# Group sums and S5 products reordered at the start, the fourth modulation group read behind the recurrence, and both layers' memory keys and values computed before the first FFN

## The chip, the cores and the metric

The kernel runs on one core of a Trainium2 chip. The metric is the device time of one execution in microseconds. A profiled execution gives a span and a record of every instruction and transfer; the times of this text come from there unless they are called medians.

## The reference

Two transformer blocks work on 512 tokens of 1024 channels. The first is modulated by a vector c, and mixes with four branches (RWKV-7, spatial gating, short convolution, S5). The second has two layers of attention with 12 heads, and 4 heads more that attend to 256 memory tokens. Cut to what matters:

```python
mod = silu(c) @ ada_w + ada_b                     # 1024 x 6144
sh1, sc1, gt1, sh2, sc2, gt2 = split(mod, 6)
h = rms_norm(x, g1) * (1 + sc1) + sh1
p = h @ w_in
merged = sum(sigmoid(gate_i) * branch_i(p))       # four branches
x = x + gt1 * (merged @ w_o)
h = rms_norm(x, g2) * (1 + sc2) + sh2
x = x + gt2 * (relu(h @ ffn_w1) ** 2 @ ffn_w2)
x = rms_norm(x, final_g)
for layer in (0, 1):                              # fox attention, dilated attention
    xn = rmsnorm(x, norm_mix[layer])
    mn = rmsnorm(mem, norm_mem[layer])            # 256 memory tokens
    q, k, v, qm = split(xn @ w_in_2[layer])       # layer 0: and the forget logits
    km, vm = split(mn @ w_mem_kv[layer])
    heads = concat(attention(q, k, v), softmax(qm @ km.T / 8) @ vm)
    x = x + heads @ w_out[layer]
    x = x + conv_ffn(rmsnorm(x, norm_ffn[layer]))
out = rmsnorm(x, norm_final)
```

## The kernel before

**Products.** Activations lie channels by tokens, in eight k-blocks of 128 channels. A product is split: each weight and each activation is a high and a low part, and three matmuls (w_hi h_hi, w_hi h_lo, w_lo h_hi) stand for one. A weight piece has 1024 columns of 128 rows; for a tile of 128 channels by 512 tokens it gives 24 matmuls (L1617). POOL loads pieces in a fixed order into four slots: w_hi by one transfer two pieces ahead (L442), a negated copy (L448), then a second transfer that adds the weight to it (L451), which makes w_lo. The first load waits until DVE has used two modulation blocks (L453). PE's tiles go through four banks of PSUM in turn; each is freed by the engine that reads it.

**Modulation.** The 1024 x 6144 matrix comes as 48 blocks of 512 KB, eight for each of the six groups. SP issues them in program order among its other transfers (L352, L357). Blocks 0 to 3 go to PE directly (L1690). For all others DVE multiplies a block by a column of silu(c) and adds it to a running sum (L576, L578 in `modulate(group, a, b)`); a MEMSET (L580) marks the end of a group; PE adds the sum over the partitions (L1682, `modulation`); DVE adds the bias (L587). Eight slots hold the first 16 blocks. Blocks 8 to 11 wait until PE has taken a slot, 12 to 15 until DVE has.

**Opening.** ACT squares x, PE adds the squares (L1841), DVE takes the reciprocal (L527). DVE then makes the S5 tables by complex products (L1009 to L1014), the last with 1024 columns, which is the S5 filter f; PE transposes it (L1850) and multiplies it (L1855). After the first two groups the norm gives h_hi (ACT) and h_lo (DVE, L534), and PE makes ten tiles of the projection: bg, cg, z of the convolution, gating and S5. DVE reads group 2 between those tiles, makes the convolution's y (L1062 to L1065), then the S5 tables (L1076 to L1092), then the spatial gating: means (L1098), squares (L1101), which PE adds (L1873), the root, and normed values (L1106) that PE multiplies (L1879). Then the S5 inputs (L1899), the RWKV recurrence, and the gates.

**Behind the recurrence.** SP issues blocks 24 to 27 when the recurrence is over, then x anew as each pair of merged tiles is ready (L412), then blocks 28 to 47. Each gated tile is a PE product, then L1127 and L1136 on DVE; the merged tiles go through w_o, eight tiles. `mixer_update(k)` (L1188) adds tile k to x and reads two blocks, of groups 3 and 4. The sums of group 3 stand on PE before w_o's last tile, those of group 4 after it, then the squares of x (L1698), and the FFN with four groups of 16 tiles.

**Heads of the two attention layers.** PE makes memq0, memq1, q0, k0, v0, then memk0, memk1, memv0, memv1: 256 columns wide, from `memory_norm` on DVE (L836, L483, L484, eight times), which norms the memory for that layer; memT is loaded for each layer. memv tiles are copied by ACT and turned by PE (L1711), and copied by DVE (L822). In the first layer DVE also makes the forget parts (L858 to L867) there. In the second q0 and k0 are rotated (L805 to L807, PE turns them by L1708). Attention starts with the memory heads: scores (L1782), maxima (L890), exponentials, turns (L1797), outputs (L1811); the other projections run beside it. The squares of the memory are made beside the last FFN groups before each layer.

The order of the work is written out by hand: each engine runs its own program, and semaphores hold it.

Of the kernel before, what the change touches and what calls it, by code (L numbers as in the profile page):

```python
# [43 lines left out]
ADA_PE, ADA_FIRST = 4, 8  # L44


def ada_landed(q):

    if q < 16:
        return f"ada_in{q % ADA_FIRST}", 16 * (q // ADA_FIRST + 1)  # L50
    return f"ada_in{q % ADA}", 32 + 16 * ((q - 16) // ADA + 1)
# [3 lines left out]
N_KV = 4  # L55


def down_pieces(first):

    pairs, cols, at = set(), {}, first  # L60
    for n_in in (N_FOX, N_DIL):
        at += n_in + N_KV
# [66 lines left out]
HEAD_PIECES = ["memq0", "memq1", "q0", "k0", "v0", "memk0", "memk1", "memv0", "memv1"]  # L129
# [22 lines left out]
def turned_pieces(layer):  # L152

    return [name for name in HEAD_PIECES + BESIDE_PIECES if name[0] == "v" or name[:4] == "memv" or (layer and name[0] in "qk")]
# [18 lines left out]
def build(nc, A, out):  # L173
    n_mixer = sum(n for _, n in mixer_pieces())
    n_block1 = n_mixer + 8 + 2 * 8 * FF_GROUPS
    small_extra = 3 * sum(n for what, n in mixer_pieces() if what.endswith("_out"))
    pair_first, piece_cols = down_pieces(n_block1)
    first_beside = n_block1 + small_extra + 1 + len(HEAD_PIECES)
# [9 lines left out]
    pieces = n_block1 + sum(n + N_KV + 8 + 2 * FF2 + 8 * len(FF2_GROUPS) for n in (N_FOX, N_DIL))  # L188
    with ExitStack() as ctx:
# [80 lines left out]
        first_slots = [arena[:, at:at + D] for at in [base_at + D * i for i in range(ADA_FIRST - 2)] + [4096, 4096 + D]]  # L270
# [40 lines left out]
        mem_in = at_m["p"].rearrange("p a b c -> p (a b c)")[:, 0:KT * MT].rearrange("p (k t) -> p k t", k=KT)  # L311
# [5 lines left out]
        room = at_m["pt"].rearrange("p a b c -> p (a b c)")  # L317
        mem_sq = lambda k: room[:, MT * (k % 2):MT * (k % 2) + MT]
        mem_t = lambda k: room[:, MT * (2 + k % 2):MT * (2 + k % 2) + MT]
        mem_total, mem_rstd = room[:, 4 * MT:5 * MT], room[:, 5 * MT:6 * MT]  # L320
# [11 lines left out]
        def mn(pair, k):  # L332

            return pair[:, k // 2, MT * (k % 2):MT * (k % 2) + MT]
# [4 lines left out]
        def _(sp):  # L339
# [22 lines left out]

# [7 lines left out]
            for q in range(16, 24):  # L370
                ada_piece(q, ada_second["ada"])
# [1864 lines left out]
```

## Time and profile before

| | us |
|---|---|
| median of the runs (lowest to highest, 3 runs) | 2261.84 (2259.82 to 2265.03) |
| the profiled execution | 2262.56 |
| its span | 2260.7 |
| PE busy | 2124.0 (94%) |
| DVE busy | 1296.8 (57%) |
| POOL busy | 841.6 (37%) |
| ACT busy | 455.7 (20%) |

The mean granted clock of PE was 0.968 of full speed. A profile lists busy time and, before a group of instructions, the idle time of its engine with what ended it. An engine that is not the bound may be idle without a price; what counts is which wait ends last in a stretch. A busy PE is not always a fast one, since its clock has two levels, 1.2 and 2.4 GHz.

### The profile page before, as it was taken

To read this page: it belongs to the slowest core of one execution; us is meant where nothing else is said; L and a number is where in the kernel's file an instruction comes from. 1 tells how busy PE (TensorE), PEld (TensorE's weight loads), DVE (VectorE), ACT (ScalarE), POOL (GpSimd) and SP (SyncE) were. 2 spreads that over 40 slices of the span, in tenths; PEclk is the share of its full clock that TensorE was granted. 3 is DMA by queue.
4 is the path that set the end of the run, shared out by engine and by line. 5 is a ranking of instruction groups with operands and counts; after the bars stand their busy time and mean duration, and the time that the engine had idled before them with its cause. 6 is when DMAs were issued, how large, how long until landed. Compare 5 with 4: busy or idle time off the path is not lost.

```text
span 2260.7 us, 27381 instructions
## 1 busy us (share of the span) xinstructions
PE 2124.0 (94%) x10790; PEld 1684.3 (75%) x10790; DVE 1296.8 (57%) x1827; ACT 455.7 (20%) x839; POOL 841.6 (37%) x1009
## 2 busy tenths in 40 slices
PE   6989799998799999998999999999989989999996
PEld 5768587776588888876777888888766768888885
DVE  6775646437653243684444754727746657727374
ACT  2112301220100000313333211202224342202021
POOL 1323233233244444442223444444432224444442
PEclk7999899999799999999999999999999999999998
DMA  8867567579799888875556888988964549889885
GB/s 289 229 139 170 112 142 165 114 168 234 210 241 198 190 193 195 190 170 119 110 103 162 186 192 198 186 197 171 200 135 99 112 90 195 189 196 197 190 187 127
DMA packets 121783, 389.34 MB, mean 172 GB/s; under 512 B 25220, under 2 KB 27396, under 8 KB 121272
## 3 DMA queue, kind: packets, MB, share of 16 engines
q0 software_dynamic: 96624, 346.27, 70.6%
q1 hardware_dynamic: 25032, 41.32, 5.5%
q8 instruction: 86, 1.41, 0.3%
q14 instruction: 41, 0.34, 0.0%
HBM read 383.67 MB, written 3.92 MB: 171 GB/s over the span
## 4 chain that ended last, share of the span: by engine, by line
PE 77%; DVE 14%; DMA 6%; issue 1%; ACT 1%; POOL 0%; SPq 0%; DVEq 0%; ACTq 0%
PE ps L1617 64%; DMA w_lo<-in_w 2%; DMA arena<-in_ada 2%; PE ps L1646 2%; PE ps L1782 2%; PE ps L1811 2%; PE ps L1797 1%; DVE work L690 1%; PE ps L1969 1%; DVE g_lo L484 1%; PE ps L1733 1%; DVE arena L691 1%; DVE arena L578 1%; DMA w_hi<-in_w 1%; DVE small L890 0%
## 5 line engine op out<-in xcount | busy, mean ns | idle before, releaser
L1617 PE MATMUL ps<-h_hi,w_hi 128*128 128x512 f32 x1760 | 711.8, 404 | 27.3 <-DVE h_lo L534 13.1
L1617 PE MATMUL ps<-h_hi,w_lo 128*128 128x512 f32 x1760 | 690.3, 392 | 0.0
L1617 PE MATMUL ps<-h_lo,w_hi 128*128 128x512 f32 x1760 | 690.2, 392 | 0.0
L442 POOL DMA_DIRECT2D w_hi<-in_w x334 | 186.3, 558 | 1218.1 <-PE ps L1617 1082.9
L1617 PEld LDWEIGHTS ps<-h_hi,w_hi 128*128 128x128 f32 x1760 | 333.0, 189 | 125.5 <-issue 29.9
L1617 PEld LDWEIGHTS ps<-h_hi,w_lo 128*128 128x128 f32 x1760 | 332.8, 189 | 71.5
L1617 PEld LDWEIGHTS ps<-h_lo,w_hi 128*128 128x128 f32 x1760 | 333.8, 190 | 65.0 <-issue 2.2
L448 POOL TENSOR_SCALAR w_lo<-w_hi 128x1024 fp32r<-128x1024 f32 (+1 forms) x334 | 355.6, 1065 | 67.1 <-DMA w_hi<-in_w 61.8
L451 POOL DMA_DIRECT2D w_lo<-in_w x334 | 300.9, 901 | 106.0 <-POOL w_lo L448 106.0
L1617 PE MATMUL ps<-g_hi,w_hi 128*128 128x512 f32 (+1 forms) x760 | 297.1, 391 | 10.3 <-DMA w_lo<-in_w 6.3
L1617 PE MATMUL ps<-g_lo,w_hi 128*128 128x512 f32 (+1 forms) x760 | 291.1, 383 | 0.0
L1617 PE MATMUL ps<-g_hi,w_lo 128*128 128x512 f32 (+1 forms) x760 | 291.0, 383 | 0.0
L1617 PEld LDWEIGHTS ps<-g_hi,w_hi 128*128 128x128 f32 x760 | 144.8, 191 | 43.9 <-DMA w_lo<-in_w 9.2
L1617 PEld LDWEIGHTS ps<-g_hi,w_lo 128*128 128x128 f32 x760 | 144.7, 190 | 27.8
L1617 PEld LDWEIGHTS ps<-g_lo,w_hi 128*128 128x128 f32 x760 | 144.9, 191 | 26.6 <-issue 0.5
L1575 ACT ACTIVATE arena<-arena,vec 128x512 f32<-128x512 f32 x88 | 71.8, 816 | 392.1 <-DVE arena L936 388.8
L950 DVE TENSOR_TENSOR x<-ps,x 128x512 f32<-128x512 f32 x48 | 33.2, 692 | 146.0 <-PE ps L1617 135.8
L941 DVE SCALAR_TENSOR_TENSOR arena<-arena,vec 128x511 f32<-128x511 f32 x88 | 114.9, 1305 | 3.3 <-ACT arena L1575 0.3
L936 DVE TENSOR_TENSOR arena<-ps,work 128x512 f32<-128x512 f32 x88 | 60.8, 691 | 90.3 <-PE ps L1617 88.9
L1205 DVE TENSOR_TENSOR arena<-arena 128x512 f32<-128x512 f32 x32 | 54.3, 1696 | 70.6 <-ACT arena L1496 70.6
L1213 DVE SCALAR_TENSOR_TENSOR x<-ps,mod,x 128x512 f32<-128x512 f32 x32 | 24.0, 751 | 101.9 <-PE ps L1617 101.7
L483 DVE CAST g_hi<-arena 128x512 fp32r<-128x512 f32 (+1 forms) x100 | 75.5, 755 | 3.4
(376 smaller groups left out, 2109.3 us busy)
## 6 DMA issues: line engine op xcount, KB each, us to landing
w_hi<-in_w POOLq DMA_DIRECT2D x318, 512.0 KB, 3.9
w_lo<-in_w POOLq DMA_DIRECT2D x318, 512.0 KB, 5.6
arena<-in_ada SPq DMA_DIRECT2D x40, 512.0 KB, 9.4
w_hi<-in_w POOLq DMA_DIRECT2D x16, 384.0 KB, 3.4
w_lo<-in_w POOLq DMA_DIRECT2D x16, 384.0 KB, 5.1
x<-in_ada SPq DMA_DIRECT2D x8, 512.0 KB, 7.9
x<-in_xT SPq DMA_DIRECT2D x1, 2048.0 KB, 9.5
x<-in_xT SPq DMA_DIRECT2D x4, 512.0 KB, 5.3
```

Source lines behind the costliest of these rows:

```text
L442: pool.dma_start(w_hi[:, q % SLOTS, 0:n], A["w"][q][:, 0:n]).then_inc(S(f"high_in{q % SLOTS}"), 16)
L448: pool.tensor_scalar(w_lo[:, q % SLOTS, 0:n], w_hi[:, q % SLOTS, 0:n].bitcast(F32), -1.0, 0.0, ALU.mult, ALU.add).then_inc(S("negated"), 1)
L451: pool.dma_start(w_lo[:, q % SLOTS, 0:n], A["w"][q][:, 0:n], accum_op=ALU.add).then_inc(S(f"low_in{q % SLOTS}"), 16)
L483: do(dve.tensor_copy(hi, src))
L936: do(dve.tensor_tensor(cv_m["z"][:, side, :], tile()[:], rstd, ALU.mult), "conv_scaled")
L941: do(dve.scalar_tensor_tensor(dst[:, 1:], z[:, :T - 1], w(1), dst[:, 1:], ALU.mult, ALU.add))
L1205: do(dve.tensor_tensor(s, r, r, ALU.mult), "relu_used")
L1575: do(act.activation(c[:, j % 2, :], cv_m["z"][:, side, :], ACT.Identity, scale=V("cw2", at), bias=V("cb2", 44 * layer + 22 * side + j0 + j ...
L1617: mm = pe.matmul(bank, w[:, slot, cols], a(k), start=(k == 0 and i == 0), stop=(k == blocks - 1 and i == 2))
L1646: mm = pe.matmul(banks[i], w[:, slots[i], cols], a(k), start=(k == 0 and j == 0), stop=(k == blocks - 1 and j == 2))
L1782: mm = pe.matmul(ps[2 + g][:, 0:width], at_m["q"][half(g), pair, P * qb:P * qb + P], keys, start=True, stop=not fox)
L1811: mm = pe.matmul(ps[6][64 * g:64 * g + 64, P * qb:P * qb + P], values, at_m["pt"][:, u % 2, g, P * b:P * b + P], start=(b == 0), stop=(b = ...
```

## The change

1. **Opening.** Eleven blocks have their own slots and are issued at once; the other five wait for DVE's reads alone. DVE's filter product stands behind the norm, `modulate(1)` ahead of the reciprocal. PE makes three tiles of the projection before the S5 transposes (other banks) and one between those and the S5 products.
2. **Group 2.** Blocks 16 to 19 are issued at h_ready, 20 to 23 behind the S5 transfers. DVE reads them beside the S5 and RWKV steps; the convolution's y moves into the gating's waits; PE's sums of the group, in a bank of the tiles, stand ahead of the gate projections.
3. **Group 3.** Blocks 24 to 27, memT and 28 to 31 are issued behind the recurrence; DVE reads the group after o_normed and after rw_out. x is loaded behind them. `mixer_update(k)` reads one block, of group 4.
4. **Memory.** Both layers' memory keys and values are made between w_o and the first FFN, from one load of memT. The factor 1/rms of a memory token is applied afterwards: to keys on DVE, in the first FFN group; to values by ACT as it copies them. Values are made tokens by channels, so nothing is turned. The heads lose memory_norm, four pieces, their copies and turns; v0's turn moves into attention.

The core of the diff:

```diff
-ADA_PE, ADA_FIRST = 4, 8
+ADA_PE, ADA_FIRST = 4, 11
...
             for q in range(16):
-                if ADA_FIRST <= q < ADA_FIRST + ADA_PE:
-                    sp.wait_ge(S("ada_taken"), q - ADA_FIRST + 1)
-                elif q >= ADA_FIRST + ADA_PE:
-                    sp.wait_ge(S("ada_used"), q - ADA_FIRST - ADA_PE + 1)
-                sp.dma_start(first_slots[q % ADA_FIRST], A["ada"][q]).then_inc(S(ada_landed(q)[0]), 16)
+                if q >= ADA_FIRST:
+                    sp.wait_ge(S("ada_used"), q - ADA_FIRST + (3 if q == 15 else 1))
+                sp.dma_start(first_slots[first_room(q)], A["ada"][q]).then_inc(S(ada_landed(q)[0]), 16)
...
             def memory_root():
                 need("rms_ready")
                 do(dve.reciprocal(mem_rstd, mem_rstd))
+                for i in range(2):
+                    do(dve.tensor_tensor(mem_m["diag"], mem_rstd[:, P * i:P * i + P], K("ident"), ALU.mult))
+                    do(dve.tensor_reduce(mem_row[:, i:i + 1], mem_m["diag"], AX.X, ALU.add), "mem_row")
+            def memory_low(i):
+                layer, k = i // KT, i % KT
+                need("mem_high")
+                do(dve.scalar_tensor_tensor(mn(g_lo, layer, k), mem_in[:, k, :], V("g_mem2", 8 * layer + k), mn(g_hi, layer, k).bitcast(F32),
+                                            ALU.mult, ALU.subtract), "mem_ready")
...
-            complex_product(f, (by_step(0, 0), by_step(1, 0)), (by_channel(bb[:, 0]), by_channel(bb[:, 1])), blocks4(tmp))
...
             modulate(0, ADA_PE, 8)
+            modulate(1, 0, 8)
             norm_start()
-            modulate(1, 0, 8)
             modulation(0, 2)
...
+            complex_product(f, (by_step(0, 0), by_step(1, 0)), (by_channel(bb[:, 0]), by_channel(bb[:, 1])), blocks4(tmp))
...
             def mixer_update(k):
                 do(dve.scalar_tensor_tensor(x[:, k, :], tile()[:], mod[:, 16 + k:17 + k], x[:, k, :], ALU.mult, ALU.add), "x_done")
-                modulate(3 + k // 4, 2 * (k % 4), 2 * (k % 4) + 2)
+                for i in range(3 * k, min(3 * k + 3, 2 * KT)):
+                    memory_low(i)
+                if k == 2:
+                    memory_root()
+                modulate(4, k, k + 1)
...
             branch_out(3, 8)
+            for k in range(KT):
+                pe.wait_ge(S("mem_square"), k + 1)
+                pe.matmul(PB[:, 0:MT], K("ones"), mem_sq(k), start=(k == 0), stop=(k == KT - 1)).then_inc(S("mem_square_used"), 1)
             project(7, "x_done", ready=lambda k: need("merged"))
             modulation(3)
             project(1, "x_done")
+            memory = [(lambda k: mn(g_hi, 0, k), lambda k: mn(g_lo, 0, k)), (lambda k: mn(g_hi, 1, k), lambda k: mn(g_lo, 1, k))]
+            pe.wait_ge(S("mem_ready"), 2 * KT)
+            project(1, "mem_copied", operand=memory[0], width=MT)
             modulation(4)
+            total_squares(work[:, 2, :])
+            project(NMP - 1, "mem_copied", operand=memory[0], width=MT)
+            memory_values(0)
+            project(NMP, "mem_copied", operand=memory[1], width=MT)
+            memory_values(1)
             g = (of(g_hi), of(g_lo))
             hidden = lambda k: need("hidden")
-            total_squares(work[:, 2, :])
...
-                project(1, "dve_freed", operand=mem, width=MT, ready=lambda k: need("mem_ready"))
-                turn("v0", layer)
-                project(NMP - 1, "dve_freed", operand=mem, width=MT)
-                for i in range(NMP):
-                    project(1, "v_copied", operand=mem, width=MT)
-                    if i:
-                        turn(f"memv{i - 1}", layer)
-                turn(f"memv{NMP - 1}", layer)
-                attention(layer)
+                attention(layer, ready)
```

`memory_values(layer)` opens two weight pieces; for each of eight k-blocks and two halves of the memory tokens it issues three matmuls, 256 columns wide, with the memory as the stationary operand.

**The order on DVE in the opening**, from the S5 filter on (`arena` holds modulation blocks and S5 tables; L1009 to L1014 are one complex product). Before:

```order
L1012 TENSOR_TENSOR arena<-arena 128x1024
L1013 TENSOR_TENSOR arena<-arena 128x1024
L1014 TENSOR_TENSOR arena<-arena 128x1024
L1033 TENSOR_SCALAR arena<-arena 128x128
L576 TENSOR_SCALAR arena<-arena,small 128x1024
L578 SCALAR_TENSOR_TENSOR arena<-arena,small 128x1024 x3
L580 MEMSET small 128x8
L527 RECIPROCAL work<-work 128x512
L576 TENSOR_SCALAR arena<-arena,small 128x1024
L578 SCALAR_TENSOR_TENSOR arena<-arena,small 128x1024 x7
L580 MEMSET small 128x8
L587 TENSOR_TENSOR mod<-ps,vec 128x16
```

Now:

```order
L597 TENSOR_SCALAR arena<-arena,small 128x1024
L599 SCALAR_TENSOR_TENSOR arena<-arena,small 128x1024 x3
L601 MEMSET small 128x8
L597 TENSOR_SCALAR arena<-arena,small 128x1024
L599 SCALAR_TENSOR_TENSOR arena<-arena,small 128x1024 x7
L601 MEMSET small 128x8
L548 RECIPROCAL work<-work 128x512
L608 TENSOR_TENSOR mod<-ps,vec 128x16
L1036 SCALAR_TENSOR_TENSOR small<-mod,vec 128x8
```

The six products of 1024 columns and the scaling by -1 stand behind the norm's sixteen steps now, and the reciprocal behind both groups' reads.

**The order on SP behind the recurrence** (`ada` are modulation blocks). Before:

```order
L357 DMA arena<-in_ada 128x1024 [waits ada_used,rec_o]
L357 DMA arena<-in_ada 128x1024 [waits ada_used] x3
L412 DMA x<-in_xT 128x1024 [waits merged] x4
L357 DMA arena<-in_ada 128x1024 [waits ada_used] x20
L416 DMA arena<-in_memT 128x2048 [waits ada_used]
```

Now:

```order
L365 DMA arena<-in_ada 128x1024 [waits ada_used,rec_o]
L365 DMA arena<-in_ada 128x1024 [waits ada_used] x3
L420 DMA arena<-in_memT 128x2048
L365 DMA arena<-in_ada 128x1024 [waits ada_used] x4
L425 DMA x<-in_xT 128x1024 [waits merged] x4
L365 DMA arena<-in_ada 128x1024 [waits ada_used] x16
```

memT and the second half of group 3 stand before the reload of x; sixteen blocks are left behind it.

## Rows read from the trace of the kernel before

**Rows 1.** The page, part 1: busy us, share of the span, instructions.

```profile
PE 2124.0 (94%) x10790; PEld 1684.3 (75%) x10790; DVE 1296.8 (57%) x1827; ACT 455.7 (20%) x839; POOL 841.6 (37%) x1009
```

**Rows 2.** Waits of PE: line, releaser: us in total, times, longest.

```profile
PE ps L1617 <- DVE h_lo L534: 13.1, 7, 6.8
...
PE ps L1873 <- DVE arena L1101: 7.3, 1, 7.3
...
PE ps L1879 <- DVE arena L1106: 1.7, 2, 1.1
```

**Rows 3.** Windows: us; PE, PEld, DVE, ACT, POOL busy; clock; DMA share; GB/s.

```profile
20.00:25.00 5.00, 5.00 (x29) 3.22 (x27) 4.83 (x6) 3.10 (x4) 0.00 (x0) 1.00 0.25 95
25.00:30.00 5.00, 5.00 (x33) 5.00 (x32) 4.83 (x6) 0.00 (x0) 0.00 (x0) 0.67 0.64 210
...
40.00:45.00 5.00, 5.00 (x39) 4.96 (x37) 4.70 (x4) 0.56 (x2) 1.45 (x2) 0.50 1.06 312
```

**Rows 4.** Chain that ended last, opening: start, us, what.

```profile
34.48 14.23 DMA arena<-in_ada
```

**Rows 5.** Timeline of DVE, opening: start, us, operation, tiles, count [idle before].

```profile
20.30 1.23 DVE L1009 TENSOR_TENSOR arena<-arena 128x1024 f32<-128x1024 f32 x1
...
37.49 7.31 DVE L578 SCALAR_TENSOR_TENSOR arena<-arena,small 128x1024 f32<-128x1024 f32 x5
...
48.80 1.63 DVE L578 SCALAR_TENSOR_TENSOR arena<-arena,small 128x1024 f32<-128x1024 f32 x1 [1.42 <-DMA arena<-in_ada]
```

**Rows 6.** Timeline of PE, opening to the spatial gating.

```profile
32.27 3.66 PE L1850 MATMUL ps<-con,arena 128*128 128x128 f32 x16
35.85 7.01 PE L1855 MATMUL ps<-arena 64*128 64x16 f32 x64
...
50.62 3.58 PE L1682 MATMUL ps<-con,arena 128*128 128x1 f32 x16 [4.25 <-DVE small L580]
...
141.82 3.78 PE L1873 MATMUL ps<-arena,con 128*128 128x512 f32 x4 [7.28 <-DVE arena L1101]
```

**Rows 7.** Timeline of DVE behind the recurrence: the first gated tile.

```profile
519.25 0.69 DVE L1127 TENSOR_TENSOR work<-ps,arena 128x512 f32<-128x512 f32 x1 [4.18 <-PE ps L1617]
```

**Rows 8.** Window of w_o, columns as in rows 3.

```profile
541.60:586.80 45.20, 43.30 (x187) 34.94 (x187) 28.66 (x29) 4.44 (x7) 17.66 (x21) 0.96 0.98 297
```

**Rows 9.** Timeline of PE, from w_o to the first FFN.

```profile
567.39 0.50 PE L1617 MATMUL ps<-h_hi,w_hi 128*128 128x512 f32 x1 [1.14 <-DMA w_lo<-in_w]
...
573.81 0.50 PE L1617 MATMUL ps<-h_hi,w_hi 128*128 128x512 f32 x1 [0.68 <-DMA w_lo<-in_w]
...
590.90 3.57 PE L1682 MATMUL ps<-con,arena 128*128 128x1 f32 x16 [4.05 <-DVE small L580]
```

**Rows 10.** Chain that ended last: the first FFN tiles, and those behind.

```profile
607.32 57.11 PE ps L1617 x234
...
666.11 261.30 PE ps L1617 x1152
```

**Rows 11.** Timeline of PE, memory products of both layers.

```profile
997.78 0.28 PE L1617 MATMUL ps<-g_hi,w_hi 128*128 128x256 f32 x1
...
1634.13 1.02 PE L1708 MATMUL ps<-arena,con 128*128 128x512 f32 x2
...
1642.53 0.56 PE L1617 MATMUL ps<-g_hi,w_hi 128*128 128x256 f32 x1
...
1651.09 0.39 PE L1617 MATMUL ps<-g_hi,w_hi 128*128 128x256 f32 x1 [1.64 <-DMA w_lo<-in_w]
```

**Rows 12.** Timeline of DVE, heads of both layers.

```profile
1011.06 1.77 DVE L858 TENSOR_SCALAR work<-work 12x512 f32<-12x512 f32 x1
...
1018.02 0.68 DVE L867 TENSOR_TENSOR work<-work 12x512 fp32r<-12x512 f32 x1
...
1021.73 0.69 DVE L890 TENSOR_REDUCE small<-ps 128x2 f32<-128x512 f32 x1 [1.48 <-PE ps L1782]
...
1657.16 0.69 DVE L890 TENSOR_REDUCE small<-ps 128x2 f32<-128x512 f32 x1 [1.09 <-PE ps L1782]
```

More of the change, by code:

```diff
@@ L152, in turned_pieces @@
 def turned_pieces(layer):
-    return [name for name in HEAD_PIECES + BESIDE_PIECES if name[0] == "v" or name[:4] == "memv" or (layer and name[0] in "qk")]
+    return [name for name in HEAD_PIECES + BESIDE_PIECES if name[0] == "v" or (layer and name[0] in "qk")]
 TURNED = [turned_pieces(layer) for layer in range(2)]
@@ L186, in bank_of @@
         return tile % BANKS
-    pieces = n_block1 + sum(n + N_KV + 8 + 2 * FF2 + 8 * len(FF2_GROUPS) for n in (N_FOX, N_DIL))
+    pieces = n_block1 + sum(n + 8 + 2 * FF2 + 8 * len(FF2_GROUPS) for n in (N_FOX, N_DIL))
     with ExitStack() as ctx:
@@ L1208, in ffn_group @@
                         modulate(5, j, j + 1)
-                    if last:
-                        add_square(j, mem_sq, mem_total)
+                    if first and j < 2 * NMP:
+                        keys = mem_keys[j // NMP][:, j % NMP, :]
+                        dve.wait_ge(S("mem_copied"), 2 * N_KV)
+                        do(dve.tensor_tensor(keys, keys, mem_rstd, ALU.mult), "mem_scaled")
                 if first:
@@ L1520, in _ @@
                     rope_copy("k0")
-                    skip(1 + NMP)
-                for i in range(NMP):
-                    value_copy(f"memv{i}", layer)
+                    skip(1)
                 before = len(UNITS) * layer
@@ L1683, in modulation @@
                                    start=(group > 0), stop=True, skip_group_check=True)
+                if group == 2:
+                    mm.then_inc(S("tile"), 1)
+                    t[0] += 1
+                    freed[at] = ("dve_freed", n.next("dve_freed"))
+                    return
                 mm.then_inc(S("ada_total"), 1)
@@ L1825, in attention @@
                     next(steps, None)
+                    if u == 0:
+                        turn("v0", layer)
                     for name, at in zip(BESIDE_PIECES, DONE_AT):
@@ L1846, in _ @@
             halves = [slice(0, 64), slice(64, 128)]
+            modulation(0)
+            modulation(1)
+            project(3, "dve_freed", ready=h_tile)
             pe.wait_ge(S("s5_f"), 1)
@@ L1927, in _ @@
             v, bd = rw_in, rw_bd
+            modulation(2)
             project(2, "gate")
@@ L2069, in _ @@
             for layer in range(2):
[L2070 to L2071 removed]
+                q_owner, ready = "rope_copied" if layer else "dve_freed", {}
                 if layer == 0:
@@ L2102, in _ @@
                     two_products(pairs, *g, "x_done", hidden)
-                    if layer == 0 and group == len(FF2_GROUPS) - 1:
-                        total_squares(mem_total, MT)
                     project(6, "x_done", operand=g, blocks=pairs)
@@ L2177, in layout @@
     stream.append(pieces_of(first["w_o"]))
+    for layer in range(2):
+        kv = i["w_mem_kv_2"][layer]
+        stream += [pieces_of(kv[:, :NMP * P]), kv[:, NMP * P:].reshape(2, 4, P, NMP * P).transpose(0, 2, 1, 3).reshape(2, P, D)]
     for g in range(FF_GROUPS):
@@ L2185, in layout @@
         memq = pieces_of(w[:, w.shape[1] - NMP * P:])
-        kv = pieces_of(i["w_mem_kv_2"][layer])
-        for m in range(NMP):
-            named.update({f"memq{m}": memq[m], f"memk{m}": kv[m], f"memv{m}": kv[NMP + m]})
+        named.update({f"memq{m}": memq[m] for m in range(NMP)})
         if layer == 0:
```

240 lines of the change are left out of this document (131 added, 109 removed).

## The prediction, made before the change was run

> **What bounds the kernel now.** I begin with the page's busy times: PE is busy for 2124.0 of 2260.7 us, no other engine for more than 1297 [rows 1]. So a change gains where PE stands idle, runs at a low clock or does work that can go. The list of PE's waits shows that the idle time is spread: 13.1 us for h_lo at the first tiles of projections, 7.3 for the spatial gating's squares, 1.7 for its normed halves [rows 2]. Each place that the change touches is then read by itself.
>
> In the **opening** PE waits for the last modulation block. It was issued at 34.48 and landed 14.23 us later [rows 4]; DVE read it, and PE began its sums at 50.62, at half clock [rows 5, 6]. Ahead of that lies a hole: from 20 to 25 us the core moved 95 GB/s with a DMA share of 0.25, from 25 to 30 us 210, against 312 when busy [rows 3]. SP holds blocks back until a place is read, and DVE is then at the S5 filter's six 128x1024 products, 1.23 us each [rows 5].
>
> **Between w_o and the FFN** PE stops 4.05 us for the fourth and fifth groups' reads [rows 9]. The first ten FFN tiles end at 664.43 [rows 10]. Ten tiles are 240 matmuls, and 261.30/1152 = 0.227 us of each is full speed, so they are worth 54.4 us: what lies before counts as ending at 610.0.
>
> In the **heads** of the two attention layers four memory pieces stand before attention. In the second, every other piece starts 8.56 us after the one two before it (1642.53 to 1651.09), and its last wait is for w_lo [rows 11]: the weights, not PE, set that pace. In the first, DVE closes the chain with the forget parts, 1011.06 to 1018.70, before the first maxima at 1021.73 [rows 12].
>
> **The change, part by part.**
>
> *Opening.* Eleven blocks are asked for at once, and the filter product, the gap's cause, stands behind the norm. Filling the hole to 312 GB/s brings (217 + 102) GB/s x 5 us = 1.6 MB forward, 5.1 us of transfer. If DVE alone set the time, its twelve blocks at 7.31/5 = 1.46 us from 20.30 on would end at 37.8, against 50.43: -12.6. I take **-7**, near the first end, because row after row of the busy stretch shows transfers as the limit, and a little beyond it because DVE no longer reads in jerks. The reciprocal now stands behind the reads, beside PE's sums, and costs nothing while those take 3.6 us.
>
> The Trainium skill ("DMA: Bandwidth & Descriptors", Queues, rings and completion order) says that a DMA engine takes turns between the queue rows that have work, packet by packet. POOL's weights start once two blocks are used, so by that rule they would now take half of the rate from blocks that before had it alone. The last block's 14.23 us with weights in flight agree in kind [rows 4]. The sum would be some 4 us higher; it is the second rival.
>
> *From the first projection to the S5 inputs.* The S5 transposes (3.66 us) and products (7.01) ran at half clock under the wait for blocks [rows 6]; now they stand between projections, at full clock 1.8 and 3.5: +5.3. What goes: the 7.28 us before L1873, since the convolution's y moves out of DVE's way to the tables; that L1873's 3.78 us ran at half clock, 1.9; the 1.7 us of L1879 [rows 2, 6]; and group 2's sums, 1.8 us at full clock by half of 3.57 [rows 9], which move. Sum **-7.4**. The rows leave room from -12, if the stalls that the first weights cause shrink too, to -4, if DVE's two convolutions, now inside the gating's waits, make L1879 late by what it loses today.
>
> *Group 2 before the gate.* The 1.8 us come back and may wait for a bank: **+2.4**, from 0 to +5. SP passes the S5 transfers with four blocks each side of them; those blocks have the S5 outputs' time to land.
>
> *Group 3 behind the recurrence.* DVE reads its eight blocks between rw_out and the first gated tile. There it now idles 4.18 us before 519.25 [rows 7]; four reads at about 1.33 are 5.3: **+1.2**. If blocks 28 to 31 land late the reads hold the gates and the price is up to +5; if they land early enough to fall into waits, 0.
>
> *w_o.* One read per update in place of two, and no second group queued. The stretch of 45.20 us ran at clock 0.96 [rows 8], so 1.8 us were lost to it, at its start behind a wait; eight memory-square products now run in that wait. Two stalls for w_lo, 1.14 and 0.68 [rows 9], come from blocks that share the transfers at 297 GB/s. Together **-3.6**. PE is then through with w_o and group 3 at 586.85 + 1.2 - 3.6 = 584.4; 586.85 is where its wait before 590.90 began [rows 9].
>
> *Memory pieces.* All eight now follow. The nearest row is the pace of the same pieces in the heads, 8.56 us for two [rows 11]: 34.2 us, and 1.3 for group 5's blocks in flight, so the FFN starts at 620.0 at full speed. The norm, the reads of group 4 and the FFN's first operand, which PE waited for until 607, lie under it; PE's idle and slow 23 us before 610.0 are the cover that this part uses. Against 610.0 it is +10.0, the two parts above included, so **+12.4** for the block alone. PE alone would need 8.56 - 1.64 = 6.92 for two: 6.6 less. With blocks in flight as in w_o, two neighbouring pieces start 6.42 apart (567.39, 573.81) [rows 9], 12.8 for two: 16 more.
>
> *Heads.* First layer: PE reached the memory pieces at 997.78 [rows 11], with v0's piece of 24 x 0.227 = 5.4 us before them, so k0 is there at 992.3 and scaled at 993.0. The forget parts' 7.7 us end at 1000.7, v0's scaling of 0.7 at 1001.4, and there the first maxima can stand: -20.3. Second: k0's turn ends at 1634.13 + 1.02 = 1635.15 [rows 11]; three steps of 0.69 and gaps are 2.2, scores and their wait 0.8, so 1638.1 against 1657.16 [rows 12]: -19.1. Together **-39.4**, give or take 4. v0's turn goes into attention, where it can cost 2 a layer if PE is the later one. The second memory load and the memory squares of the last groups go, and I put them at nothing; they lie beside PE's matmuls, and the two short additions on PE are under 1.
>
> **Sum**: -7 - 7.4 + 2.4 + 1.2 - 3.6 + 12.4 - 39.4 = -41.4, so 2262.56 - 41.4 = 2221.2 for the profiled run. The median of the runs shown lies 0.7 lower: **2220**.
>
> **Rivals.** *Memory pieces at the crowded pace*, 12.8 us for two: group 5's blocks and the weights share the transfers again. For it: the w_o rows. Against: only four blocks fit ahead. 2220 + 16 = 2236, chance 0.13. *The opening's transfers are shared and DVE's convolutions are late*: opening -3, next part -5: 2220 + 6 = 2226, chance 0.12. *More is gained*: DVE sets the opening (-5.6 more) and PE the memory pieces (-6.6): 2208, chance 0.12. *Slower*: the weight supply breaks down where eight short pieces follow one another. It needs 22 us for two, that is four times 13.4 more, 54 in all: 2274. It decides from 20 us on, where the gains are eaten (4 x 11.4 = 46). The w_o stretch, with modulation blocks and weights in flight together, shows 12.8, so 0.03. That the heads don't get shorter, because the old computation stays in them, is excluded by the rows of the order: no memory product is left there. The forecast has 0.60.
>
> **Range.** The uncertain terms together are some 12 to either side of 2220; with the rivals on both sides 2203 to 2237 leaves out the slow case and the far tails. A measurement tells about 0.2%, 4.5 us, from no change. All but the slow case and mixtures near it are faster by more: faster 0.95, same 0.02, slower 0.03.
>
> **What would show it.** In the profile after: no hole between 20 and 30 us, and PE's sums of the second group at about 44 instead of 50.62 (if later than 48, the opening's step is wrong); no wait of L1873 above 2 us; DVE ready for the first gated tile no more than 2 us after PE; memory pieces two by two at 8 to 9 us and no wait for h_lo at the first FFN tile; from attention's head to its first maxima 20 us less in both layers. Wrong if the memory pieces take over 45 us, or if first maxima come less than 15 us earlier, measured from the head's first piece.

## The result, and the profile after

The changed kernel takes 2241.78 us (median of 4 runs, 2234.45 to 2243.19) against 2260.83 for the kernel before (4 runs beside it). The ratio is 0.9909, 95% interval 0.9880 to 0.9938: about 21 us, 0.9%, faster. A second set of four runs gave 2237.94, ratio 0.9887 (0.9864 to 0.9909). Forecast were 2220 and a range of 2203 to 2237: the direction was right, the gain was about half of the forecast, and both medians lie above the range.

The page's busy times after, to be set beside [rows 1]:

```profile
PE 2121.4 (95%) x10794; PEld 1687.5 (75%) x10794; DVE 1272.3 (57%) x1778; ACT 462.0 (21%) x850; POOL 844.4 (38%) x1009
```

PE's busy time fell by 2.6 us of the 21.5 (in a second profile by 12.0 of 26.5), so most of the gain is idle time that went, and DVE has 49 instructions less. The waits of PE show what came in place of those in [rows 2]. The last line here is from the kernel before:

```profile
PE ps L1637 <- DMA w_lo<-in_w: 14.2, 9, 3.0
...
PE ps L1741 <- DMA w_lo<-in_w: 5.2, 2, 2.9
...
PE ps L1637 <- DVE h_lo L555: 4.8, 4, 3.1
...
PE ps L1933 <- DVE arena L1102: 2.6, 2, 2.0
```

```profile
PE ps L1617 <- DMA w_lo<-in_w: 12.0, 10, 2.0
```

The wait for the gating's squares is gone, that for h_lo fell from 13.1 to 4.8, and those for w_lo rose from 12.0 to 19.4 us together. (Attention's wait for ACT's exponentials, 12.1 before, is 16.3 now.) More than before, PE waits for weights.

To find where the time went I set the same events of both traces side by side (start times in us, from the timelines):

| event | before | after | gain so far | stage, measured (again) | forecast |
|---|---|---|---|---|---|
| first projection | 57.28 | 45.38 | -11.9 | -11.9 (-12.3) | -7 |
| S5 inputs | 168.35 | 154.84 | -13.5 | -1.6 (+0.1) | -7.4 |
| first product of the RWKV tables (L1969, L2024) | 278.73 | 267.08 | -11.7 | +1.9 (+1.9) | +2.4 |
| end of the recurrence | 486.36 | 478.68 | -7.7 | +4.0 (+1.4) | 0 |
| first gated tile on DVE | 519.25 | 517.92 | -1.3 | +6.4 (+5.2) | +1.2 |
| last merged tile | 541.62 | 540.96 | -0.7 | +0.7 (+0.6) | 0 |
| last update behind w_o | 586.96 | 586.15 | -0.8 | -0.2 (+0.5) | -3.6 |
| last update of the first FFN | 960.60 | 976.58 | +16.0 | +16.8 (+19.3) | +12.4 |
| first maxima, first layer | 1021.73 | 1016.84 | -4.9 | -20.9 (-20.9) | -20.3 |
| first maxima, second layer | 1657.16 | 1632.06 | -25.1 | -20.2 (-21.8) | -19.1 |
| end of the span | 2260.70 | 2239.20 | -21.5 | +3.6 (-0.3) | 0 |

"Again" is the second profile of the changed kernel against the first one of before. The heads, the largest term, came out as worked out; so did the stretch to the RWKV tables as a sum (-11.7 against -12.0). Of the 20 us that are missing in this profile most lie from the recurrence's end to the FFN: +23.7, where +10 had been forecast. The +4.0 of the recurrence and the +3.6 at the end are taken up in experiment 8.

**Opening.** Windows of the opening after (columns as in [rows 3]), DVE's reads, and POOL's first weights:

```profile
20.00:25.00 5.00, 5.00 (x19) 2.39 (x19) 3.72 (x4) 2.67 (x5) 1.86 (x4) 1.00 1.03 406
25.00:30.00 5.00, 5.00 (x32) 5.00 (x31) 4.79 (x6) 1.21 (x2) 0.98 (x2) 0.64 1.06 406
30.00:35.00 5.00, 5.00 (x25) 5.00 (x25) 3.46 (x3) 0.00 (x0) 3.78 (x5) 0.50 1.13 394
```

```profile
23.28 2.61 DVE L599 SCALAR_TENSOR_TENSOR arena<-arena,small 128x1024 f32<-128x1024 f32 x2 [0.46 <-DMA arena<-in_ada]
...
31.57 1.28 DVE L599 SCALAR_TENSOR_TENSOR arena<-arena,small 128x1024 f32<-128x1024 f32 x1 [0.80 <-DMA arena<-in_ada]
33.60 4.65 DVE L599 SCALAR_TENSOR_TENSOR arena<-arena,small 128x1024 f32<-128x1024 f32 x3 [0.74 <-DMA arena<-in_ada]
38.32 0.07 DVE L601 MEMSET small<- 128x8 f32 x1
```

```profile
23.14 1.25 POOL L452 DMA_DIRECT2D w_hi<-in_w  x2 [22.69 <-DVE arena L599]
```

The hole of 95 and 210 GB/s in [rows 3] is filled, at 394 to 406 GB/s and not at the 312 of the stretch I took as busy. The first weights are in flight from 23.1 on. DVE ends its reads at 38.3; the bound by DVE alone was 37.8.

**Behind the recurrence.** The chain of waits before, from the recurrence's end on, and after, up to the turn of the recurrence's output (L2102):

```profile
490.72 8.18 DMA w_lo<-in_w
...
498.94 5.74 PE ps L1617 x24
```

```profile
478.68 1.83 PE ps L1637 x7
...
483.04 11.04 DMA w_lo<-in_w
...
494.12 7.27 PE ps L1637 x24
501.39 2.04 PE ps L2102 x64
```

and DVE's timeline where [rows 7] stood:

```profile
511.82 5.94 DVE L599 SCALAR_TENSOR_TENSOR arena<-arena,small 128x1024 f32<-128x1024 f32 x4
517.83 0.07 DVE L601 MEMSET small<- 128x8 f32 x1
517.92 0.69 DVE L1125 TENSOR_TENSOR work<-ps,arena 128x512 f32<-128x512 f32 x1
```

Before, a w_lo of 8.18 us landed just in time: PE was busy for 12.55 of the 12.6 us up to 498.9. Now a gate piece waits for a w_lo that took 11.04 us, and PE is busy for 12.55 of 15.5. Behind that wait the granted clock is 0.77, and 24 matmuls take 7.27 us instead of 5.74. (In the second profile PE idles as long, but the clock stays at 1.00.)

**Memory pieces.** PE's waits from the end of w_o to the first FFN tile, and two windows between them (columns as in [rows 3]):

```profile
596.72 0.55 PE L1741 MATMUL ps<-w_hi,g_hi 128*128 128x256 f32 x1 [2.29 <-DMA w_lo<-in_w]
...
606.73 0.58 PE L1637 MATMUL ps<-g_hi,w_hi 128*128 128x256 f32 x1 [2.66 <-DMA w_lo<-in_w]
...
617.15 0.55 PE L1741 MATMUL ps<-w_hi,g_hi 128*128 128x256 f32 x1 [2.95 <-DMA w_lo<-in_w]
...
626.09 0.50 PE L1637 MATMUL ps<-h_hi,w_hi 128*128 128x512 f32 x1 [1.56 <-DMA w_lo<-in_w]
```

```profile
596.70:606.70 10.00, 7.35 (x48) 7.17 (x48) 1.68 (x3) 2.39 (x4) 4.99 (x6) 0.84 0.97 212
606.70:617.10 10.40, 7.47 (x48) 7.27 (x48) 7.33 (x8) 3.46 (x6) 5.02 (x6) 0.83 0.94 206
```

Here every second piece waits, and the starts are 10.0 and 10.4 us apart where 8.56 had been read in [rows 11]. In the second profile nearly every piece waits, by up to 2.57 us. From the third piece to the eighth the mean distance of two is 9.9 and 9.7 us in the two profiles. No modulation block is under way in these windows, and yet the DMA share is 0.94 to 0.97 at 206 to 212 GB/s, half of the rate of the opening.

**Heads.** DVE's rows that answer to [rows 12]:

```profile
1015.40 0.68 DVE L870 TENSOR_TENSOR work<-work 12x512 fp32r<-12x512 f32 x1
1016.11 0.69 DVE L836 TENSOR_TENSOR arena<-ps,work 128x512 f32<-128x512 f32 x1
1016.84 0.69 DVE L891 TENSOR_REDUCE small<-ps 128x2 f32<-128x512 f32 x1
...
1632.06 0.69 DVE L891 TENSOR_REDUCE small<-ps 128x2 f32<-128x512 f32 x1
```

The first maxima stand right behind the forget parts and v0's scaling, without a wait, as the prediction had them.

### The profile page after: what moved, and what is told of

Same layout as the page of the kernel before. It is cut to its first block, busy times and chain, and to the rows that moved or that the text cites. A ratio compares the mean times of both kernels' runs of the same rounds, so it can differ in the third digit from the quotient of the medians.

```text
span 2239.2 us, 27332 instructions
## 1 busy us (share of the span) xinstructions
PE 2121.4 (95%) x10794; PEld 1687.5 (75%) x10794; DVE 1272.3 (57%) x1778; ACT 462.0 (21%) x850; POOL 844.4 (38%) x1009
## 4 chain that ended last, share of the span: by engine, by line
PE 81%; DVE 10%; DMA 5%; issue 1%; ACT 1%; POOL 1%; SPq 0%; DVEq 0%; ACTq 0%
PE ps L1637 67%; DMA w_lo<-in_w 4%; PE ps L1666 2%; PE ps L1834 2%; PE ps L1863 2%; PE ps L1849 1%; DMA w_hi<-in_w 1%; PE ps L2024 1%; DVE work L711 1%; PE ps L1782 1%; DVE arena L712 1%; PE ps L1705 1%; POOL w_lo L458 1%; PE ps L1718 1%; PE ps L1894 0%
## 5 line engine op out<-in xcount | busy, mean ns | idle before, releaser
L1637 PE MATMUL ps<-g_hi,w_hi 128*128 128x512 f32 (+1 forms) x728 | 286.4, 393 | 8.4 <-DMA w_lo<-in_w 5.4
L1637 PE MATMUL ps<-g_lo,w_hi 128*128 128x512 f32 (+1 forms) x728 | 281.7, 387 | 0.0
L1637 PE MATMUL ps<-g_hi,w_lo 128*128 128x512 f32 (+1 forms) x728 | 281.7, 387 | 0.0
L1637 PEld LDWEIGHTS ps<-g_hi,w_hi 128*128 128x128 f32 x728 | 138.2, 190 | 42.1 <-DMA w_lo<-in_w 8.9
L1637 PEld LDWEIGHTS ps<-g_hi,w_lo 128*128 128x128 f32 x728 | 138.0, 190 | 27.8
L1637 PEld LDWEIGHTS ps<-g_lo,w_hi 128*128 128x128 f32 x728 | 138.1, 190 | 26.8 <-issue 0.5
L1211 DVE TENSOR_TENSOR arena<-arena 128x512 f32<-128x512 f32 x32 | 48.7, 1523 | 83.4 <-ACT arena L1528 83.4
L1528 ACT ACTIVATE arena<-ps 128x512 f32<-128x512 f32 x32 | 19.1, 597 | 289.3 <-PE ps L1637 289.3
```

Source lines behind the costliest of these rows:

```text
L1211: do(dve.tensor_tensor(s, r, r, ALU.mult), "relu_used")
L1637: mm = pe.matmul(bank, w[:, slot, cols], a(k), start=(k == 0 and i == 0), stop=(k == blocks - 1 and i == 2))
```

## The experiments

My theory after the result: the weights alone keep the DMA engines nearly busy, since each comes by two transfers, so pieces that PE does in half the time are paced by bytes; and 5 MB asked for behind the recurrence delay weights that PE needs at that moment. Rivals: the pace comes from the order in which POOL loads (room, w_hi, negation, w_lo), or from the transfers' adding; and moved blocks cost the same wherever they stand.

**1. The changed kernel again (after_again).** No edit.

> The changed kernel once more, for a second profile. Theory A (the 4 us that the recurrence stretch lost against before belong to the change): from the first L2024 matmul to the end of the recurrence it takes 211.6 us again, within 1. Rival (they are scatter of one execution): it comes back to about 207.6, the value of before. The time stays at 2234 to 2243.

The stretch took 209.0 us: neither of the two values. It is taken up again in experiment 8. The time, 2237.94, and the other stages are in the table.

**2. Half of the memory weights' bytes (mem_half).**

```diff
+    piece_cols.update({n_mixer + 8 + i: D // 2 for i in range(2 * N_KV)})
```

> Of the eight memory pieces only the first 512 of 1024 weight columns are loaded, in both transfers; the other half of each product uses what lies in the slot. PE's work is the same. Theory A (the bytes set the pace: weights alone keep the DMA engines 94 to 97% busy at 206 GB/s, 5.0 us a piece): two pieces start about 6 us apart instead of 10, PE's own time, and the run is 14 to 16 us shorter, about 2226. Rival B (the chain of room, negation, second transfer sets it, mostly latency): the landing falls from 7.2 to some 5 us, two pieces 7.5 apart, 9 to 10 us shorter, about 2232. Rival C (neither, PE waits for its operands): no change.

2231.86, 6.1 below the changed kernel's runs beside it (2237.94). From the last update of w_o to the last of the FFN it took 384.3 us instead of 390.4 and 392.9. So the bytes matter, but for less than theory A gave: pieces still waited, up to 1.54 us, while the DMA share was 0.79. The pace, 7.4 us for two in mean from the third piece to the eighth, and the time are near rival B's. This run cannot part bytes from chain, since POOL's negation is halved with them (0.64 us and not 1.06).

```profile
590.00:600.00 10.00, 9.23 (x73) 8.62 (x72) 4.89 (x5) 2.78 (x5) 5.59 (x10) 1.00 0.79 148
```

**3. Held burst (hold_burst).**

```diff
             for q in range(24, 24 + ADA):
                 ada_piece(q, ada_m["ada"])
+            sp.wait_ge(S("rw_o"), 1)
             sp.dma_start(mem_in, A["memT"]).then_inc(S("mem_in"), 16)
```

> memT and blocks 28 to 31 are issued only when PE has turned the first half of the recurrence's output. Theory A (the 5 MB burst right behind the recurrence is what delays the two gate pieces' weights): w_lo, which took 11.04 us there, lands in 7 or less, the turn at L2102 starts 3 to 4 us earlier, and most of it stays: 2 to 4 us shorter. Rival B (the same bytes only move): the gates come earlier, but DVE's reads of 28 to 31 or ACT's squares of memT end as much later, and the time is the same within 2 us, or up to 3 longer.

The turn (L2102) starts 17.9 us behind the recurrence's end, against 22.6 and 21.4, and 18.3 in the kernel before: the whole delay of the turn is due to what was held. It was no burst of 5 MB, though: in the changed kernel's trace SP issues blocks 28 to 31 only at 491.0 to 495.0, when DVE has freed their places, and what was in flight beside the late w_lo were 24 to 27 and memT, 3 MB. But the blocks then come late for DVE, in this kernel's timeline:

```profile
507.70 1.28 DVE L600 SCALAR_TENSOR_TENSOR arena<-arena,small 128x1024 f32<-128x1024 f32 x1 [1.47 <-DMA arena<-in_ada]
510.79 1.28 DVE L600 SCALAR_TENSOR_TENSOR arena<-arena,small 128x1024 f32<-128x1024 f32 x1 [1.81 <-DMA arena<-in_ada]
513.43 1.29 DVE L600 SCALAR_TENSOR_TENSOR arena<-arena,small 128x1024 f32<-128x1024 f32 x1 [1.36 <-DMA arena<-in_ada]
```

To the first gated tile it is 37.3 us (39.2 and 38.0; before 32.9). The time, 2236.92, is not to be told from the changed kernel's. Rival B holds for the sum, theory A for the cause of the turn's delay, with memT in the burst's place (experiment 6).

**4. Memory weights staged (stage_mem, stage_early, stage_dve, stage_dve_hold).** Each memory piece is fetched once by SP into a free room of the arena, and split on the chip:

```diff
+                if q in staged:
+                    room_free(q)
...
+                    pool.tensor_scalar(w_hi[:, q % SLOTS, :], stage[i], 1.0, 0.0, ALU.mult, ALU.add).then_inc(S("negated"), 1)
+                    pool.wait_ge(S("negated"), negated[0] - 1)
+                    pool.tensor_tensor(w_lo[:, q % SLOTS, :], stage[i], w_hi[:, q % SLOTS, :].bitcast(F32),
+                                       ALU.subtract).then_inc(S("negated"), 1)
...
+            for i in range(2 * N_KV):
+                sp.dma_start(stage[i], A["w"][mem_first + i]).then_inc(S(f"ada_first{i // 4}"), 16)
```

> Same result as the changed kernel by another way of loading: the eight memory pieces are fetched once, as they are, by SP behind block 39, into free rooms of the arena, and POOL makes w_hi and w_lo from them. Half of the bytes, none of them needed during the memory pieces. Theory A (bytes of the weights set the pace): two pieces start 6 us apart, 14 to 17 us shorter, about 2225. Rival B (the slots and POOL's order set the pace, not the bytes): POOL's two operations of 1 to 2 us each and the wait for room leave two pieces at 8 us or more, at most 6 us shorter.

2232.21, 5.7 shorter than the changed kernel's runs beside it: rival B's bound, and in part for its reason. In stage_mem's POOL timeline the pieces land late and take 3.5 us each:

```profile
581.99 1.05 POOL L479 TENSOR_SCALAR w_hi<-arena 128x1024 fp32r<-128x1024 f32 x1 [11.69 <-DMA arena<-in_w]
583.12 2.40 POOL L481 TENSOR_TENSOR w_lo<-arena,w_hi 128x1024 fp32r<-128x1024 f32 x1
585.49 1.06 POOL L479 TENSOR_SCALAR w_hi<-arena 128x1024 fp32r<-128x1024 f32 x1
```

From the third on the memory pieces stand 2.9 us apart on PE and not 4, but POOL comes late to the FFN's first weights, and PE waits 3.96 us for them at 622.02. stage_early issues the pieces behind blocks 35 and 39:

> As stage_mem, with the first four memory pieces fetched behind block 35 and the last four behind block 39. In stage_mem the pieces landed at 582 and POOL then needed 3.5 us for each, so that the FFN's weights came at 622. Theory A (the late landing and POOL's 3.5 us set the block there): POOL can split three pieces before w_o ends, the FFN starts at 611 to 614, 8 to 11 us shorter than stage_mem, about 2223. Rival B (the 4 MB in w_o delay its weights as much): w_o 4 us or more longer, 0 to 5 us shorter in all.

2232.79. From w_o's last update to the FFN's it is 385.3 us, 3.8 shorter, but w_o is 48.7 us, 3.0 longer: what the pieces take from w_o's weights there eats it (PE waits four times for w_lo there, 4.8 us together). That is rival B's mechanism, and a little worse than its bounds. stage_dve lets DVE subtract:

```diff
+                q = mem_first + i
+                dve.wait_ge(S("negated"), q + 1)
+                do(dve.tensor_tensor(w_lo[:, q % SLOTS, :], stage[i], w_hi[:, q % SLOTS, :].bitcast(F32), ALU.subtract), "mem_row")
```

> Same result as the changed kernel. As stage_early, but POOL makes only w_hi of the eight memory pieces (1.05 us each) and DVE subtracts it (about 1.3 us each), three pieces in the last updates of w_o and five ahead of the norm. In stage_early POOL's 3.5 us a piece and then the FFN's weights behind them set the start of the FFN at 616. Theory A (POOL's time is the last limit there): the memory pieces follow one another at PE's 2.9 us, the FFN's weights are loaded under them, the FFN starts at 606 to 610: 6 to 9 us shorter than stage_early, about 2225. Rival B (DVE's norm behind the five subtractions, or the FFN's first weights, end last): FFN at 613 or later, 0 to 3 us shorter than stage_early.

2231.91. PE then has no wait among the memory pieces, but one at the end, in its chain:

```profile
604.94 3.94 DMA w_hi<-in_w
608.97 1.47 POOL w_lo L484
610.73 5.67 DMA w_lo<-in_w
616.44 23.66 PE ps L1678 x91
```

The FFN's first weights may only be asked for when a slot is free, and their chain takes 11.5 us, longer than the three memory pieces that PE still has: rival B.

> stage_dve with memT and blocks 28 to 31 held until the first half of the recurrence's output is turned, as in hold_burst. Same result as the changed kernel. hold_burst brought 4 us at the gates and gave 2.7 back at the first gated tile. Theory A (both gains stand apart): 1 to 2 us shorter than stage_dve. Rival B (the later memT delays the memory pieces' operands, which now are needed sooner): the same or up to 3 longer than stage_dve.

2232.98: rival B, no gain on top. All four beat both kernels by their medians, and compute what the changed kernel computes: against before 0.9856 (0.9838 to 0.9875) for stage_mem and 0.9868 (0.9852 to 0.9884) for stage_dve. Among themselves they can't be told apart.

**5. Same bytes, no chain (mem_plain, mem_add_now).** For memory pieces the second transfer is issued right behind the first, once as a plain copy, once as an adding one:

```diff
                 pool.dma_start(w_hi[:, q % SLOTS, 0:n], A["w"][q][:, 0:n]).then_inc(S(f"high_in{q % SLOTS}"), 16)
+                if q in memory:
+                    pool.dma_start(w_lo[:, q % SLOTS, :], A["w"][q]).then_inc(S(f"low_in{q % SLOTS}"), 16)
```

> For the eight memory pieces the second transfer is a plain copy, issued right behind the first: no negation, no waiting for w_hi, no addition in the transfer; so w_lo holds the whole weight there and not its rest. The bytes are the same. Theory A (the bytes of plain transfers set the pace): two pieces stay about 10 us apart, no change, 2235 to 2240. Rival B (the chain of room, w_hi, negation and adding transfer, or the adding itself, sets it): the pace falls to 7 us or less, and the run is 8 to 14 us shorter, 2224 to 2230. In mem_half both seemed to act, since half of the bytes brought 6 us and not 14.

2229.9: the stretch is 382.1 us, 8 to 11 shorter with all bytes, and no memory piece waits; they stand 2.9 us apart, and PE waits only behind them, 4.42 us for the FFN's first weights. "Plain bytes set the pace" falls. In mem_plain's windows (columns as in [rows 3]) the same engines move far more:

```profile
590.00:600.00 10.00, 10.00 (x83) 9.77 (x82) 4.86 (x3) 2.61 (x6) 3.44 (x7) 1.00 0.90 306
600.00:606.00 6.00, 6.00 (x52) 6.00 (x52) 5.17 (x7) 4.06 (x7) 1.85 (x4) 1.00 1.01 355
```

> For the eight memory pieces the second, adding transfer is issued right behind the first, without the negated copy that it should add to, so w_lo holds another sum there. The bytes and the adding are those of the changed kernel, only the chain (w_hi landed, negation, then the second transfer) is gone. mem_plain, which had neither chain nor adding, was 8 to 10 us shorter in this stretch. Theory A (the adding transfers hold the DMA engines about twice as long as plain ones, 4.8 us a piece for both): two pieces stay 9 to 10 us apart and the run is within 2 us of the changed kernel, 2236 to 2242. Rival B (the chain sets the pace): as mem_plain, 2226 to 2232.

2236.92, within theory A's bounds by the time, though not by the pace. Its windows, and PE's waits:

```profile
590.00:600.00 10.00, 9.56 (x75) 8.88 (x74) 5.20 (x5) 2.16 (x5) 4.28 (x6) 1.00 1.02 259
600.00:610.00 10.00, 7.55 (x59) 7.17 (x60) 6.76 (x9) 5.35 (x9) 1.96 (x3) 1.00 1.08 269
```

```profile
604.79 0.39 PE L1645 MATMUL ps<-g_hi,w_hi 128*128 128x256 f32 x1 [1.72 <-DMA w_lo<-in_w]
608.65 0.36 PE L1749 MATMUL ps<-w_hi,g_hi 128*128 128x256 f32 x1 [0.74 <-DMA w_lo<-in_w]
612.25 0.39 PE L1749 MATMUL ps<-w_hi,g_hi 128*128 128x256 f32 x1 [0.49 <-DMA w_lo<-in_w]
621.28 0.80 PE L1645 MATMUL ps<-h_hi,w_hi 128*128 128x512 f32 x1 [5.90 <-DMA w_lo<-in_w]
```

With adding the share is 1.02 to 1.08 at 259 to 269 GB/s, and the pieces that wait are 3.6 to 4.9 us apart. From the third piece to the eighth the mean distance of one is 2.9 us with neither chain nor adding, 3.7 with adding alone, and 4.9 to 5.0 with both, in the two profiles of the changed kernel: adding costs transfer time, and the chain costs the rest. Both act; my split of 4.8 us a piece for the transfers alone was too high. The share of 0.94 to 0.97 in the changed kernel did not mean full engines either, since the same transfers without the chain moved a quarter more. The time in all hardly fell, for two reasons. w_o got 3.4 to 4.0 us longer: the adding transfers start earlier and delay its last weights (one w_lo took 10.63 us). And the FFN's first weights come last, with a wait of 5.90 us (1.56 and 2.86 in the changed kernel).

**6. Group 3 back in w_o (g3_back).**

```diff
-                modulate(3, 0, 4)
...
-                modulate(3, 4, 8)
...
-                modulate(4, k, k + 1)
+                modulate(3 + k // 4, 2 * (k % 4), 2 * (k % 4) + 2)
```

> Group 3 is fetched and read as in the kernel before, two blocks in each update of w_o, with group 4; all else as in the changed kernel. Theory A (what part 3 takes in front of w_o it does not give back in w_o): from the end of the recurrence to the first gated tile 35 us instead of 39, w_o as long as it is now or 1 to 2 longer, because DVE reads two blocks in each update and group 4 ends later; in all 0 to 4 us shorter than the changed kernel. Rival B (part 3 pays in w_o): w_o and the wait for group 4's sums get 5 us or more longer, in all 2 to 6 longer.

2241.2. To the first gated tile 37.1 us, 1 to 2 less than with part 3, but w_o takes 48.2 instead of 45.2 and 45.8, and PE waits 6.34 us for group 4's last read. Rival B by the stages, though somewhat smaller. By them part 3 pays, by little; the time, which lies in the changed kernel's range, does not show it. The turn is late here as well (22.5 us behind the recurrence), with 24 to 27 and memT alone in flight; with 24 to 27 alone, in hold_burst, it was 17.9. So the 1 MB of memT is enough.

**7. Less traffic in w_o (hold_g5, pace_w_o).**

```diff
-            for q in range(24 + 2 * ADA, 48):
+            for q in range(24 + 2 * ADA, 40):
+                ada_piece(q, ada_m["ada"])
+            sp.wait_ge(S("hidden_relu"), 1)
+            for q in range(40, 48):
                 ada_piece(q, ada_m["ada"])
```

> Blocks 40 to 47 are issued only when the first FFN tile is read, so that none of group 5 is in flight in w_o and in the memory pieces. Theory A (in w_o the next group's blocks take the place of those that were moved ahead, which is why w_o did not get shorter): the last tiles of w_o and the first memory pieces come 2 to 4 us earlier, and the FFN's first group hides group 5: 2 to 4 us shorter. Rival B (w_o is limited by something else): w_o takes its 45 us again, same time; and if the FFN does not hide the late group 5, up to 4 us longer.

2241.07, w_o 45.4 us: rival B. Group 5's blocks, which I had held to be w_o's new burden, cost nothing. Instead I spread the first four blocks of group 4:

```diff
+                if 32 < q < 36:
+                    sp.wait_ge(S("x_done"), q - 32)
                 ada_piece(q, ada_m["ada"])
```

> Blocks 33 to 35 are issued one per update of w_o instead of all at once behind the reload of x; all else as in the changed kernel. Theory A (the four blocks issued together at 541 us are what delays w_o's weights, whose w_hi and w_lo took 8.6 and 8.9 us there): the two waits for w_lo of 0.8 and 1.1 us and the half clock behind them go, w_o is 1 to 3 us shorter, and so is the run. Rival B (weights and blocks share the same transfers in any order, and the reads of blocks 32 to 35 then hold the updates): w_o the same or up to 3 us longer.

w_o took 43.8 us, 1.4 to 2.0 shorter. PE's two waits for w_lo are still there; what is gone is the low clock at the start of w_o, 1.00 here against 0.91 in both profiles of the changed kernel:

```profile
559.50 0.50 PE L1639 MATMUL ps<-h_hi,w_hi 128*128 128x512 f32 x1 [0.91 <-DMA w_lo<-in_w]
571.88 0.50 PE L1639 MATMUL ps<-h_hi,w_hi 128*128 128x512 f32 x1 [1.20 <-DMA w_lo<-in_w]
```

```profile
541.20:560.20 19.00, 18.03 (x78) 14.55 (x79) 10.71 (x17) 3.38 (x6) 8.47 (x9) 1.00 0.96 273
```

So theory A's waits did not go, and only its second part came. It is one profile: w_o took 44.4 to 45.8 us in profiles whose w_o was not touched, and 2238.77 against 2237.94 and 2241.78 is no difference that these runs can tell.

**8. The kernel before, twice more (before_again, before_third).** No edit.

> The kernel before once more, for a second profile. Open is whether the stretch from the first L1969 matmul to the recurrence's end (207.6 us in the first profile of before, 207.4 to 212.2 in the profiles with the changed order, whose code there is the same) and the one from the second layer's first maxima to the end (603.5 against 601.2 to 607.9) belong to the change. Theory A (scatter of single executions): before too comes out up to 4 us away from its first profile in one of them, anywhere in 207 to 212 and 601 to 608. Rival B (the change costs some 2 us in the first): 207.6 again within 0.5.

> As before_again, a third profile of the kernel before: Theory A (scatter): the two stretches differ again by 1 us or more from one of the other two profiles. Rival B (2 us belong to the change): the first stretch is 207.6 again within 0.5.

The first stretch took 210.4 and 210.7 us here, against 207.6 in the first profile of before: theory A. The +4.0 and +1.4 of the table are scatter, most of it that first profile's. The last stretch was 604.6 and 604.3 (603.5 first), and 601.2 to 607.9 in the changed orders: scatter as well, as far as these profiles go.

## Why the prediction was right or wrong

With three profiles of before and two after the stages are, in mean: to the RWKV tables -11.2, recurrence +0.7, to the gates +5.9, merging +0.6, w_o -0.8, memory pieces and FFN +18.0, first head -20.7, second layer's head with what lies before it -20.4, rest +1.1: together about -27. (The medians differ by 19 and 25; one of the three profiles of before was a long one.) Forecast was -41.4. Some 13 of the 15 us between them lie in three terms: group 3 behind the recurrence, w_o, and the memory pieces.

**Opening: right in kind, too small.** "Near the first end, because transfers are the limit" failed. The busy stretch I took as the rate, 312 GB/s, had adding transfers of weights in it; up to 30 us blocks and plain first weights together moved at 406, and from 35 to 40, with w_lo in flight, the rate was 287. So the blocks came sooner, and the reads ended near DVE's bound of 37.8. That they ended just there is partly luck: the bound took 1.46 us for each read, where most now took 1.31, and DVE waited 2.75 us for blocks, in four places. The Trainium skill's page "DMA: Bandwidth & Descriptors" (Queues, rings and completion order) says that a DMA engine takes turns between the queue rows that have work. The trace agrees in kind: from 24.5 to 30.5 us SP's queue, with the blocks, had a DMA share of 0.71 and POOL's, with the weights, 0.35. That is a third and not half, and the part did not get 4 us longer, as the rival had it.

**To the S5 inputs: too large.** The waits went as listed, but the clock did not follow: the windows from 45.4 to 75.4 and to 105.4 ran at 0.92 and 0.89, where the 60 us behind the first projection of before had 0.94 and 1.00. The S5 products, 64 matmuls of 16 columns, took 4.40 us and not 3.5, at a granted clock of 0.83; in the 5.2 us behind them it was 0.50, and 25 matmuls there took 8.44. The steps "at full clock 1.8 and 3.5" left that out. That both misses cancel is luck.

**Group 2: right**, +1.9 by the trace.

**Group 3: the failed step is that only DVE's reads were counted.** I had asked what the reads cost behind rw_out: 2.0 us, where I said 1.2 (16.6 us from the turn to the first gated tile in both profiles, 14.6 in the three of before). I did not ask who else was loading when blocks and memT are issued: POOL, for the gate pieces in the same 15 us. Experiments 3 and 6 show the other 4 of the 5.9 us, and that memT is what did it.

**w_o, -0.8 for -3.6: neither of the two losses went.** The waits for w_lo were 0.81 and 1.11 us (1.14 and 0.68 before), and the clock from 541 to 560 was 0.91 (0.90 before). That the waits "come from blocks that share the transfers" is not borne out: eleven blocks were issued in w_o in place of 14, and PE waited 1.9 and 3.0 us in the two profiles, against 1.8 to 2.6 in the three of before; spread out (pace_w_o) they still left 2.1. Four places are empty when w_o begins, so SP issues four blocks at once, at 541.4 to 542.8, where before they came one or two at a time from 547.1 on. Spreading them gave the clock back in the one profile of pace_w_o. What delays w_lo there stays open, and DVE's 6.56 us wait for x was not tried.

**Memory pieces: the term that was mis-sized, +18.0 for +12.4.** The pace of 8.56 us came from a head in which PE had waited for DVE, so that slots were full when the row began; it was no steady pace. POOL's row of before shows it, with an idle wait for a free slot:

```profile
1643.39 0.56 POOL L442 DMA_DIRECT2D w_hi<-in_w  x1 [4.97 <-PE ps L1617]
```

Steady it is 9.7 to 9.9 for two. By experiment 5 adding transfers, which moved fewer GB/s than plain ones at the same share, and the chain in which they stand set it together. The prediction's own sign, memory pieces over 45 us, did not come: they took 40.2 and 41.4. Rival one of the prediction (blocks in flight at 12.8) did not happen; it was nearest in time, for another reason.

**Heads: right**, in mean both within 1.5 us, since those chains were made of rows of engines and needed no transfer.

**The chance.** The rivals on the side of less gain named one or two places each. Three small misses in the stretch from 478 to 626 us, two of them in its transfers, came to 13 us together, nearly the 16 of the largest of those rivals, and I had let them stand as independent.

## What to carry to other kernels

When work is moved into a stretch, list every queue's transfers of that stretch with their rate and share before and after; a transfer that delayed nothing in its old place can delay others in the new one, as the 1 MB of memT did. A pace read from a row counts only if no buffers had been filled ahead when the row began. And where a weight is split by two transfers, one of them adding, short products can be paced by loading: fetching once and splitting on engines that idle gave some 6 us here, until the next weights' chain became the limit.

## What was not expected of the hardware

Weight loads of which every second one adds into SBUF moved 206 to 212 GB/s at a DMA share of 0.94 to 0.97 in the changed kernel, and 259 to 269 at 1.02 to 1.08 when no chain held them, where transfers of the same weights without the addition moved 306 to 355 at 0.90 to 1.01, and modulation blocks with the first plain weights 406 (20 to 30 us). And POOL needed 2.40 us to subtract two tiles of 128x1024, DVE 1.24 (stage_dve's chain):

```profile
587.65 1.24 DVE w_lo L1218
```
